# Side input of the gated embedding loaded during the gate batches, its norm two slabs later

## The reference, cut to what matters

```python
for i in range(DEPTH):
    ...
    h = h + peer(rms_norm(h, ln_ffn_g[i]), peer_wq[i], peer_subkeys[i], peer_u[i], peer_v[i])

    e = rms_norm(p[i] @ ple_wp[i], ple_norm_g[i])
    h = h + jax.nn.sigmoid(h @ ple_wg[i]) * e

def peer(...):          # for each token, the experts that its product keys pick
    h = jnp.einsum('md,med->me', xb, u_tab[ib])
    return jnp.einsum('me,med->md', gb * jax.nn.gelu(h, approximate=False), v_tab[ib])
```

## Time and profile before

| what | value |
|---|---|
| median of 3 runs (lowest, highest) | 3596.24 us (3586.27, 3596.98) |
| the profiled execution's own time | 3603.66 us |
| its span, first to last instruction | 3601.9 us |
| PE busy, mean granted clock | 97%, 0.979 |
| DVE, ACT, POOL busy | 78%, 43%, 35% |
| HBM traffic over the span | 225 GB/s mean |

### The profile page before, as it was taken

How to read it: one execution, slowest core, us unless ns; L and a number is a source line. 1 busy time by engine, 2 the same in 40 slices (tenths; PEclk the granted TensorE clock), 3 DMA queues, 4 the chain that set the end, 5 groups by cost and what they waited for, 6 DMA issues and landing times.

```text
span 3601.9 us, 60313 instructions
## 1 busy us (share of the span) xinstructions
PE 3479.1 (97%) x19944; PEld 3272.4 (91%) x19944; DVE 2793.9 (78%) x5784; ACT 1530.9 (43%) x2319; POOL 1270.0 (35%) x1052
## 2 busy tenths in 40 slices
PE   8999999999998999999999899999999989999998
PEld 6877799999998999998988778999999989999997
DVE  7357588888887888888673676888988879888885
ACT  4334433336664333333443444333466643333333
POOL 0000001218775446666000000111277745566640
PEclk9999999999999999999999999999999999999999
DMA  4200244458889999999422002444588899999992
GB/s 147 76 18 1 70 135 145 143 164 292 291 298 361 377 386 371 389 372 375 140 94 82 7 1 83 152 146 151 182 294 298 296 384 387 375 380 371 378 354 76
DMA packets 266843, 814.19 MB, mean 226 GB/s; under 512 B 24880, under 2 KB 107056, under 8 KB 263088
## 3 DMA queue, kind: packets, MB, share of 16 engines
q1 hardware_dynamic: 93168, 339.06, 26.4%
q0 software_dynamic: 73728, 268.47, 19.8%
q10 hardware_dynamic: 99776, 204.50, 15.7%
HBM read 709.17 MB, written 102.76 MB: 225 GB/s over the span
## 4 chain that ended last, share of the span: by engine, by line
PE 66%; DMA 16%; DVE 8%; issue 4%; POOL 4%; ACT 1%; DVEq 1%; ACTq 0%; SPq 0%
PE bank L447 17%; PE bank L448 17%; PE bank L449 17%; DMA gath<-slabs,rows_of 10%; DMA gath<-u_rows,rows_of 6%; PE bank L1499 5%; POOL gath L622 3%; PE bank L1262 2%; DVE acc L2174 1%; DVE wlo L444 1%; PE bank L506 1%; PE bank L482 1%; PE bank L1455 1%; DVE act_w L2135 1%; PE bank L1366 1%
## 5 line engine op out<-in xcount | busy, mean ns | idle before, releaser
L444 DVE TENSOR_TENSOR wlo<-raw,whi 128x1024 fp32r<-128x1024 f32 x628 | 793.4, 1264 | 359.0 <-ACT whi L398 329.4
L447 PE MATMUL bank<-act_hi,whi 128*128 128x384 f32 (+1 forms) x2848 | 1011.5, 355 | 4.4 <-ACT stage L974 2.2
L448 PE MATMUL bank<-act_lo,whi 128*128 128x384 f32 (+1 forms) x2848 | 999.7, 351 | 0.0
L449 PE MATMUL bank<-act_hi,wlo 128*128 128x384 f32 (+1 forms) x2848 | 999.6, 351 | 0.0
L398 ACT ACTIVATE whi<-raw 128x1024 fp32r<-128x1024 f32 x628 | 666.2, 1061 | 525.9 <-PE bank L449 500.1
L447 PE MATMUL bank<-w_hi,whi 128*128 128x384 f32 x2048 | 696.2, 340 | 45.7 <-DVE w_lo L2140 45.6
L448 PE MATMUL bank<-w_lo,whi 128*128 128x384 f32 x2048 | 691.8, 338 | 0.0
L449 PE MATMUL bank<-w_hi,wlo 128*128 128x384 f32 x2048 | 691.2, 337 | 0.0
L614 POOL TENSOR_TENSOR onehot<-onehot,cidx 128x800 f32<-128x800 f32 x56 | 123.9, 2244 | 1472.6 <-DVEq L2025 1472.6
L622 POOL DMA_INDIRECT gath<-slabs,rows_of x256 | 483.4, 1888 | 295.8 <-DVE acc L2174 254.1
L447 PEld LDWEIGHTS bank<-act_hi,whi 128*128 128x128 f32 x2848 | 538.0, 189 | 37.6 <-ACT stage L974 2.6
(11 more groups left out here) (324 smaller groups left out, 4025.3 us busy)
## 6 DMA issues: line engine op xcount, KB each, us to landing
raw<-slabs SPq DMA_DIRECT2D x636, 512.0 KB, 4.4
hidden_dram<-hst ACTq DMA_DIRECT2D x256, 192.0 KB, 3.3
gates_dram<-stage ACTq DMA_DIRECT2D x24, 2048.0 KB, 7.5
h_sb<-hidden_dram ACTq DMA_DIRECT2D x64, 768.0 KB, 8.4
g_sb<-gates_dram ACTq DMA_DIRECT2D x32, 1536.0 KB, 20.7
gath<-u_rows,rows_of POOLq DMA_INDIRECT x256, 7.8
gath<-slabs,rows_of POOLq DMA_INDIRECT x256, 8.5
res<-x_t SPq DMA_DIRECT2D x2, 1024.0 KB, 6.8
```

The lines of the kernel that those rows point to most:

```text
L444: nc.vector.tensor_tensor(wlo[k][:], raw[k][:], whi[k][:].bitcast(F32), ALU.subtract).then_inc(s_slab_lo, 1)
L447: nc.tensor.matmul(out, a_hi, b_hi, start=first, stop=False)
L448: nc.tensor.matmul(out, a_hi, b_lo, start=False, stop=False)
L449: return nc.tensor.matmul(out, a_lo, b_hi, start=False, stop=last)
```

## The change

The three tiles of the side input move to the address of `g_sb0`, the buffer for V's first gates, which is unused until those are loaded. The load of `p_sb` is issued by ACT ahead of the first gate batch. `p_hi` is made in stage 0 and not 1. The first load of gates moves from stage 4 to 6 (the matmuls of slabs 4 and 5 read `p_hi` and `p_lo` at its address), the second from 12 to 14. The norm's sums go behind slab 13 instead of 11, its root and reciprocal from stage 12 to 14, its spread behind slab 15 instead of 13, the scaling of `e_t` to stages 16 and 17, and `weigh`, `w_high` and `w_low` for V's first slabs two stages later as well. `p_lo`, the squares and their folds stay where they are. No instruction is added or removed but one wait.

```diff
-        p_sb = place("p_sb", [P, 2, T], F32, m)
-        p_hi = place("p_hi", [P, 2, T], F32R, m)
-        p_lo = place("p_lo", [P, 2, T], F32R, m)
+        m = [m[0] + 3 * 2 * T * 4]
...
         h_sb = [place(f"h_sb{i}", [P, HB, TD], F32, m) for i in range(2)]
+        mp = [m[0]]
+        p_sb = place("p_sb", [P, 2, T], F32, mp)
+        p_hi = place("p_hi", [P, 2, T], F32R, mp)
+        p_lo = place("p_lo", [P, 2, T], F32R, mp)
         g_late = place("g_sb0", [P, TD // TG, GB, TG], F32, m)
...
                 act.wait_ge(S["selt_copied"], NT)
+                act.dma_start(p_sb[:], p_t[layer]).then_inc(S["p_loaded"], 16)
                 gap_rows(0, 0, 0)
...
-                    if x == 0:
-                        act.wait_ge(S["gm_ready"], 2 * TD // 8 + 4)
-                        act.dma_start(p_sb[:], p_t[layer]).then_inc(S["p_loaded"], 16)
...
-                    if x == 4:
+                    if x == 6:
                         act.wait_ge(S["stored_a"], TD // TG // 2 * 16 + 1)
                         act.wait_ge(S["stored_b"], TD // TG // 2 * 16 + 1)
                         load_g(0, 0)
-                    if x == 1:
+                    if x == 0:
                         act.wait_ge(S["p_loaded"], 16)
                         nc.scalar.activation(p_hi[:], p_sb[:], ACT.Copy).then_inc(S["p_hi_ready"], 1)
...
-                    if x == 12:
+                    if x == 14:
                         norm_std(act, "ple", 1, 1.0 / D)
                         load_g(1, 1)
-                    if x in (13, 14):
-                        w_high(x - 13, x - 13)
+                    if x in (15, 16):
+                        w_high(x - 15, x - 15)
...
-                    if x == 11:
+                    if x == 13:
                         norm_sums(pe, "ple", 1, e_sq)
-                    if x == 13:
+                    if x == 15:
                         norm_spread(pe, "ple", 1)
...
-                    if x == 12:
+                    if x == 14:
                         norm_rs(dve, "ple", 1)
-                    if x in (14, 15):
+                    if x in (16, 17):
                         dve.wait_ge(S["rstd_bc"], bc_seen("ple") + 1)
```

More of the change, by code:

```diff
@@ L2152, in _ @@
                         fold_squares(dve, "ple", e_sq, range(2 * x - 13, min(2 * x - 11, KD)))
-                    if x == 12:
+                    if x == 14:
                         norm_rs(dve, "ple", 1)
-                    if x in (14, 15):
+                    if x in (16, 17):
                         dve.wait_ge(S["rstd_bc"], bc_seen("ple") + 1)
-                        for k in range(4 * (x - 14), 4 * (x - 14) + 4):
+                        for k in range(4 * (x - 16), 4 * (x - 16) + 4):
                             V.scalar_tensor_tensor(e_t[:, k, :], e_t[:, k, :], par[:, Q_PLE + k:Q_PLE + k + 1], bank[5][:],
                                                    ALU.mult, ALU.mult).then_inc(S["e_scaled"], 1)
-                    if x == 13:
+                    if x == 15:
                         weigh(0, 0, 0, 0, 0)
                         weigh(1, 1, 0, 0, 0)
-                    if x == 14:
+                    if x == 16:
                         w_low(0, 0)
                         weigh(2, 2, 0, 0, 0)
-                    if x == 15:
+                    if x == 17:
                         w_low(1, 1)
```

## The result

Before 3596.21 us (median of 20 runs, 3580.62 to 3612.59), after 3609.59 us (20 runs, 3600.81 to 3622.49). The ratio is 1.0037 with a 95% interval of 1.0023 to 1.005. The change costs 13.4 us; the prediction had +2.8 and a range of 3580 to 3610, whose upper end is 0.4 us above what was measured.

The account below looks back on a forecast made before the run. DVE, held by the gathers, was taken as slower than TensorE through the tail, so the stall only moves to the spread. V's door +1.1 and +1.7 us, together +2.8 on 3596.2, gave 3599 us, range 3580 to 3610.

Parts of the forecast that it names:

- forecast's own mechanism: Tail: TensorE's stall moves from the norm's sums to the spread, DVE no faster; 3599 us, 3589 to 3607, chance 0.62.
- The two waits and their sizes: Tail: TensorE's 4.7 us wait for the sums goes; a 6.7 us wait for `rs` appears at the spread.
- The load of p is worth 1.3 us at dot 5: Early tail: p's 0.52 MB leaves the gathers' way, so dot 5 and `p_lo` come 1.3 us earlier.
- rs at 81.2 and 80.0: DVE behind dot 29: the reciprocal is ready at 1182.6 us in layer 1 and 2962.8 in layer 2.
- slower rival: First gates load from stage 6 delays the gathers, 3.8 us a layer, 3607 us; decides above 11 us a turn; chance 0.15.
- DVE's way from rs to the scaling, 14.3 us: DVE, stages 15 to 17: dots, `weigh`, split and four scalings after `rs` take 14.3 us, ending at V's door.
- V's door is +1.1 and +1.7: V's tenth matmul, which needs all of `e_t` scaled, comes 1.1 us later in layer 1, 1.7 in layer 2.
- The slow clock behind the spread is hidden: Slabs 16 and 17: at most 2.85 us of slow clock; TensorE's 11.2 us stays beneath DVE's 12.7.
- The faster rival: Tail: gathers need only TensorE's 8.33 us a turn, DVE keeps up, the stall goes for good; 3575 us, chance 0.23.
- That the change does nothing: Tail: only p's bytes leave and the norm's gain is lost at V's door; 3594 us, inside the main range.
- The gates' load hidden by TensorE's slack: Stage 9's GELU, held by an `hst` store behind the gates load: up to 4 us free, costed at nothing.
- The rule weighed: DMA in the tail: the skill's HBM limit of about 358 GB/s was set aside for the trace's 410 GB/s.

Follow-up runs that it names:

- e7: The change itself measured again in another session for a second profiled execution: 3614.11 us, 1.0048 of the kernel before.
- e2: Kernel before with only the norm, weighing and second gates load two stages later; side input and first gates load as before: 3608.0 us, 1.0036.
- e6: e2 with dots 28 to 31 moved behind the scaling, to the end of stages 16 and 17: 3592.75 us, 0.9978 of the kernel before.
- e9: Kernel before with only the first load of V's gates moved from stage 4 to 6: 3601.24 us against 3600.95, 1.0002.
- e12: The kernel of e6 measured again: 3599.86 us against 3603.33 for the kernel before, 0.9989.
- e3: The change, but DVE makes `rs` between stage 14's two dots instead of behind both: 3620.93 us, 1.0071 of the kernel before.
- e1: The change with only its side-input part and first gates load kept; norm, weighing and second gates load in old stages: 3599.87 us against 3596.57 before, 1.0019.
- e5: The change with dots 28 to 31 moved behind the scaling, to the end of stages 16 and 17: 3601.43 us, 1.0005 of the kernel before.

## Why the prediction came out as it did

The time was inside the stated range, but by 0.4 us, and above the 3589 to 3607 of the forecast's own mechanism. A loss of 0.37% is beyond the 0.3% that the prediction called distinguishable, an outcome to which it gave 0.15. e7 measured the same kernel at 3614.11 us, outside the range. So that the range held is in part luck: the sum was short by 10.6 us.

*The two waits and their sizes.* Right: the sums' wait is gone from both layers, and one for `rs` stands at the spread, 8.6 and 9.1 us (4.6 and 7.7 in e7) where 6.7 was forecast, with a slow slab 16.

*The load of p is worth 1.3 us at dot 5.* Wrong in effect. Dot 5 came at 17.8 and 18.3 against 18.0 and 17.3, and `p_lo` was waited for by 3.3 and 3.8 us against 3.1 and 1.2. The bytes of p did leave the tail. But ACT's wait for p had also held back the two loads of `h_sb`. In layer 1 they are now issued 8.9 and 13.0 us into the tail, and not 12.1 and 14.2, while the gathers of dots 4 and 5 (issued at 4.2 and 6.1) are on their way. That they are what took the gain back is argued from these rows; no run isolated it. The sign is the other way in all runs together: in the seven profiles with the early load dot 5 stands at 17.7 on average and `p_lo` is waited for by 3.2 us, in the five with p loaded in the tail and `p_lo` in its old place (before, e2, e6, e9, e12) at 17.0 and by 2.0 us.

*rs at 81.2 and 80.0.* It came at 86.2 and 87.7. Here lies the miss. 1.1 and 2.3 us of it are dot 5, later than forecast: p's missing gain, and 1.0 more in layer 2. The next 1.9 and 1.6 us are the five turns from dot 5 to 25. Beside them stands the first load of gates, which the prediction costed at nothing and left to its slower rival: the second table gives three turns of 31.6 us instead of 29.8, 1.8 us later (e9, which moves this load alone, has 30.9 and 31.4), of which 0.8 comes back in the two turns ahead. The rival had named 3.8 us and its own counterweight, and about half of it was real. Its threshold of 11 us a turn was not reached (10.5), so as a mechanism of its own it did not decide. The last part is the turn to dot 29, 2.2 and 4.1 us above the carried-over length, beside the second load of gates. In e7, the same kernel, this turn took 9.9 and 11.7 us, so most of this part belonged to the first execution. The Trainium skill, DMA: Bandwidth & Descriptors, section Queues, rings and completion order, says that each DMA engine takes turns between the queues with work. The rows agree so far as the gather issued 0.1 us behind the load released its dot 11.25 us later, against a median of 7.8; that packets alternate no run here shows.

*DVE's way from rs to the scaling, 14.3 us.* It measured 15.1 and 14.8, and 17.2 and 16.6 in e2. **This step failed in kind**: it took the durations of stage 15 from a place where both of its dots found their gathers landed, and treated the way as DVE work behind `rs`. But dot 31 lies on it, and dot 31 has a gather of its own. Where the chain is not held at dot 29 it is held at dot 31, and where `rs` comes sooner (e2, e3) the way grows. What is constant is the distance from dot 31 to the door: 12.07 to 12.09 us in all twelve tails that keep the order of the change, whatever `rs` and the stalls did. Read so, the prediction's doors of 95.5 and 94.3 put dot 31 at 83.4 and 82.2. It came at 89.2 and 90.5 in the change, 86.4 and 88.3 in e7, and 84.1 and 85.4 in e2.

*V's door is +1.1 and +1.7.* The rule, that the later of TensorE and DVE's scaling sets it, was right. The size was 6.9 and 9.9, in e7 4.1 and 7.8. The two differences are small remainders of large sums, so each microsecond of dot 31 went into them whole.

*The slow clock behind the spread is hidden.* Right: TensorE reached V's first slab and still waited, 1.7 and 2.2 us.

*The faster rival* is excluded: from dot 5 to 25 a turn took 10.9 and 10.8 us and not 8.3. DVE did not become faster, and the wait for it only moved. *That the change does nothing* is excluded by the interval. *The gates' load hidden by TensorE's slack*, up to 4 us: right; the wait for `hst` at slab 11, which the prediction had named as a sign against itself, is there, but 0.6 us in layer 2 of the change, and the 3 us of e9 cost nothing.

*The rule weighed*, about 358 GB/s for a core against the 410 of the rows: in the section that the prediction cites, the Trainium skill (DMA: Bandwidth & Descriptors, section Bandwidth) also says that each core gets about 358 GB/s when both cores on one memory domain stream. One core ran here, so the row's 410 GB/s and that sentence don't conflict, and going by the row was right.

What stays open: the medians say +13.4 us, the doors +11.8 to +16.8, but e2 has a door of +6.6 and a loss of 11.4 (3608.0 less 3596.57). One profile of a kernel can't say whether its door is typical. V adds its own spread: TensorE waits there for `w_lo` by 45.6 us in before and 37.5 in after, and by 37.5 to 64.2 over all profiles, so a trace of the tail doesn't tell how much of a later door V passes on. And what the side input's part costs by itself, between nothing and 0.4% by e1 and 8.7 us by e5 against e6, was split no further than e9.

## What to carry to other kernels

Ask of a wait that is to be removed which engine is late, and what that engine still has to do before the next meeting point. Moving the meeting later gives the early engine time and the late one none, and here it put four more DMA-bound operations in front of work that the next stage needed. Find the last operation that waits for the outside (here dot 31 and its gather), and cost the path from its landing. And a duration read where its input had already landed is no price for the same work once it stands on that path.

## What the runs showed of the hardware

**The DMA engines stay busy where the chain stalls.** The windows of after over the same 36 us of the tail as the second of the earlier trace rows, and over its 96 us (columns as there):

```profile
1107.68:1143.68 36.00, 31.94 (x151) 28.63 (x150) 21.32 (x30) 14.85 (x25) 15.55 (x12) 0.91 0.96 354
1099.04:1195.04 96.00, 83.32 (x438) 79.70 (x439) 66.69 (x96) 37.58 (x55) 41.70 (x32) 0.91 0.99 371
```

354 GB/s where before had 410. The two halves of those 36 us, and the 15 us up to the late dot 29 and just past it, say where:

```profile
1107.68:1125.68 18.00, 14.71 (x64) 13.11 (x63) 10.97 (x15) 4.31 (x6) 8.29 (x6) 0.81 1.02 405
1125.68:1143.68 18.00, 17.22 (x89) 15.52 (x88) 10.35 (x16) 10.54 (x19) 7.26 (x7) 1.00 0.90 304
1171.04:1186.04 15.00, 6.39 (x37) 6.07 (x36) 9.12 (x14) 4.76 (x6) 5.73 (x5) 0.79 1.02 396
```

The drop is in the second half alone, which in before held the first load of gates (issued at 1118.92) and in after gets it only at 1134.50; e9, which moves nothing but this load, has 365 and 377 GB/s there where before has 410 in both layers. While DVE waits for dot 29 the share is 1.02 and the rate 396 GB/s. So DVE waits for gathers while the engines are full, and the prediction's reading of the share holds at the stall. That a late dot lowers the traffic is not shown.

**The clock after a wait.** In the 36 us around slabs 4 and 5 the granted clock was 1.00 in before, 2.4 GHz throughout, and 0.91 in after, so part of them ran at 1.2 GHz. In after the first matmul of slab 4 took 0.80 us behind a wait of 3.29, and the 4 us from it on were granted 0.50. But e3 has 0.79 behind a wait of 2.48 in layer 2, and before had a wait of 3.1 in layer 1 and kept its clock, with 0.50 us for that matmul. Over all profiles, the early load of p has 0.79 or 0.80 us there in 13 of 14 tails, behind waits of 2.3 to 4.4 us, and p loaded in the tail (the same five kernels as above) has 0.50 us in 9 of 10, behind waits of 1.2 to 3.1. So the length of a wait alone does not tell whether the clock falls.
